# One 512-column product for the high part of U against both parts of x2, with the halves added afterwards, in a decoder layer's expert stage

## What is computed

```
q = (x @ w_pq)                      # 8 heads, two halves of 128
s1, s2 = q . sub_keys               # 128 scores each
idx, g = top 16 of the 256 sums of the two top-16 lists; g = softmax(top)
h = expert_u[idx] . x
a = g * gelu(h)
y = sum over the 8*16 picked of a * expert_v[idx]
```

## Time and profile before

| | before |
|---|---|
| median of 3 runs | 2499.41 us (2499.28 to 2500.96) |
| the profiled execution | 2502.8 us |
| its span | 2501.0 us |
| TensorE busy | 2409.1 us, 96% of the span |
| VectorE busy | 1548.8 us, 62% |
| ScalarE busy | 1019.1 us, 41% |
| GpSimd busy | 567.5 us, 23% |
| mean granted TensorE clock | 0.985 of full speed |

### The profile page before, as it was taken

One profiled execution on the slowest core, in us unless ns is written; L12 is line 12 of the kernel. 1 busy time (PEld: TensorE's weight loads), 2 busy tenths in 40 slices (PEclk: granted clock), 3 DMA queues, 4 the chain that ended last, 5 costly groups with the idle time before them and its releaser, 6 DMA issues.

```text
span 2501.0 us, 44448 instructions
## 1 busy us (share of the span) xinstructions
PE 2409.1 (96%) x14090; PEld 2158.2 (86%) x14090; DVE 1548.8 (62%) x2397; ACT 1019.1 (41%) x1586; POOL 567.5 (23%) x344
## 2 busy tenths in 40 slices
PE   7999999998999799999999999999799999999996
PEld 7988799877988699888889999999688888888885
DVE  4444566646434545777778888888355555555556
ACT  3444556533433342111134444444344444444442
POOL 0000000000110201777678788800000000000000
PEclk9999999999999899999999999999899999999998
DMA  8788554565444474777777777766766666666664
GB/s 308 251 277 272 165 152 135 165 239 168 158 145 161 144 180 104 154 151 153 151 155 182 184 182 183 182 183 182 205 214 218 217 218 213 219 216 219 213 220 139
DMA packets 342695, 473.74 MB, mean 189 GB/s; under 512 B 83153, under 2 KB 230865, under 8 KB 339313
## 3 DMA queue, kind: packets, MB, share of 16 engines
q1 hardware_dynamic: 301344, 446.81, 58.9%
q0 software_dynamic: 40592, 25.45, 6.4%
q10 hardware_dynamic: 704, 0.75, 0.1%
HBM read 451.77 MB, written 21.10 MB: 189 GB/s over the span
## 4 chain that ended last, share of the span: by engine, by line
PE 94%; DVE 2%; ACT 1%; issue 1%; SPq 1%; DMA 1%; POOL 0%; DVEq 0%; ACTq 0%; POOLq 0%
PE ps L660 28%; PE ps L638 18%; PE ps L427 18%; PE ps L433 15%; PE ps L627 13%; SPq L386 1%; PE ps L575 1%; PE ps L593 1%; DMA weight_ring<-in_w_in_dram 0%; DVE split_ring L1085 0%; PE ps L611 0%; DVE parts L1077 0%; ACT parts L719 0%; ACT split_ring L736 0%; PE ps L506 0%
## 5 line engine op out<-in xcount | busy, mean ns | idle before, releaser
L660 PE MATMUL ps<-parts,temp_parts 128*128 128x512 f32 x3072 | 701.0, 391 | 17.8 <-DVE parts L1407 17.8
L660 PEld LDWEIGHTS ps<-parts,temp_parts 128*128 128x128 f32 x3072 | 579.6, 189 | 139.0 <-issue 18.4
L1085 DVE TENSOR_TENSOR split_ring<-weight_ring,split_ring 128x1024 fp32r<-128x1024 f32 x288 | 353.0, 1233 | 389.0 <-ACT split_ring L736 381.1
L1054 POOL DMA_INDIRECT gates_scratch<-sbg x256 | 496.6, 1940 | 250.9 <-issue 132.6
L1407 DVE TENSOR_TENSOR parts<-region,parts 128x512 fp32r<-128x512 f32 x512 | 330.5, 687 | 288.0 <-ACT parts L944 287.9
L638 PE MATMUL ps<-parts,u_hi 128*128 128x256 f32 x2560 | 461.1, 283 | 0.3 <-DVE u_lo L1299 0.3
L736 ACT ACTIVATE split_ring<-weight_ring 128x1024 fp32r<-128x1024 f32 x288 | 303.2, 1059 | 370.0 <-PE ps L427 226.1
L427 PE MATMUL ps<-split_ring,parts 128*128 128x512 f32 x1920 | 439.9, 391 | 5.6 <-DVE parts L1201 3.9
L427 PEld LDWEIGHTS ps<-split_ring,parts 128*128 128x128 f32 x1920 | 360.8, 188 | 81.0 <-DVE split_ring L1085 4.1
L638 PEld LDWEIGHTS ps<-parts,u_hi 128*128 128x128 f32 x2560 | 399.4, 192 | 0.5 <-DVE u_lo L1299 0.5
L1293 DVE STREAM_TRANSPOSE u_turned<-u_raw 128x1024 f32<-128x1024 f32 x256 | 318.3, 1244 | 128.9 <-PE ps L627 43.1
(11 more groups left out here) (191 smaller groups left out, 956.9 us busy)
## 6 DMA issues: line engine op xcount, KB each, us to landing
u_raw<-in_peer_u_dram SPq DMA_DIRECT2D x1024, 128.0 KB
region<-in_peer_v_dram SPq DMA_DIRECT2D x256, 512.0 KB, 4.2
weight_ring<-in_w_in_dram SPq DMA_DIRECT2D x96, 512.0 KB, 5.1
weight_ring<-in_w_mkv_dram SPq DMA_DIRECT2D x64, 512.0 KB, 3.8
gates_scratch<-temps POOLq DMA_DIRECT2D x16, 1024.0 KB, 7.4
weight_ring<-in_w_o_dram SPq DMA_DIRECT2D x32, 512.0 KB, 3.9
weight_ring<-in_w_mq_dram SPq DMA_DIRECT2D x32, 512.0 KB, 3.6
weight_ring<-in_w_mo_dram SPq DMA_DIRECT2D x32, 512.0 KB, 3.6
```

The source lines that it names most:

```text
L660: m = nc.tensor.matmul(ps[:, 4 * t + q, :], e[:, c], v, start=first and n == 0, stop=False, skip_group_check=True)
L1054: pool.indirect_dma_start(gates_by_one, bass.IndirectOffsetOnAxis(ap=idx_all[:, j:j + 1], axis=0), gate_all[:, j:j + 1], None, compute_op= ...
L1085: nc.vector.tensor_tensor(w_lo[j % SPLIT], raw[j % RAW], w_hi[j % SPLIT].bitcast(F32), ALU.subtract).then_inc(lo_ready, 1)
```

## The change

`x_parts` is one tile over the two neighbouring regions that held the high part (`p1`) and the low part (`p3`) of x2, so that for each column group k an operand `x_both[:, k]` of 2 x 256 columns can be named: 256 of the high part, and 256 of the low part, which lie 4096 elements further on. In `split_unit`, `u_hi` multiplies both in one product of 512 columns: the high part's result goes to the bank's columns 0 to 255, the low part's to columns 256 to 511. `u_lo*x_hi` stays as it is and adds into columns 0 to 255. A unit is now 16 products, eight of 512 columns and eight of 256.

The two halves must be added. `take_hidden` is replaced, for the split blocks, by three steps: ACT copies columns 0 to 255 to `E` (`take_first`), DVE adds columns 256 to 511 (`add_halves`), ACT applies gelu in place (`take_summed`). The new semaphores `s_taken` and `s_summed` link them; `gelu_ready` is now given by the third step.

```diff
--- before.py
+++ after.py
@@ -101,7 +101,9 @@
                 5: RING + 6 * RC}
         TA = RING + 7 * RC
         r0, r1, r2, r3, r4, r5, r6 = [at(f"region{n}", HOME[n], RC) for n in range(7)]
-        p0, p1, p3, p4 = [at(f"parts{n}", HOME[n], RC, F32R) for n in (0, 1, 3, 4)]
+        p0, p4 = [at(f"parts{n}", HOME[n], RC, F32R) for n in (0, 4)]
+        x_parts = at("x_parts", HOME[1], 2 * RC, F32R)
+        p1, p3 = x_parts[:, 0:RC], x_parts[:, RC:2 * RC]
         ring = at("weight_ring", 0, RING)
         ta = at("temps", TA, TEMPS)
         ta_parts = at("temp_parts", TA, TEMPS, F32R)
@@ -150,6 +152,7 @@
         u_lo = [at(f"u_lo{s}", HOME[5] + (US + s) * UW, UW, F32R) for s in range(US)]
         u_hi = [at(f"u_hi{s}", HOME[5] + (2 * US + s) * UW, UW, F32R) for s in range(US)]
         xw = r0
+        x_both = x_parts[:, :].rearrange("p (n k t) -> p k n t", n=2, k=KB)
         E = at("experts", 0, NKEY * T)
         HALF, QTR = D // 2, D // 4
         v_raw = [r5[:, s * HALF:(s + 1) * HALF] for s in range(4)]
@@ -266,12 +269,12 @@
         top_ready, gexp_ready, gate_ready = sem("top_ready"), sem("gexp_ready"), sem("gate_ready")
         u_landed = [sem(f"u_landed{s}") for s in range(US)]
         u_turned, u_hi_ready, u_lo_ready, u_used = sem("u_turned"), sem("u_hi_ready"), sem("u_lo_ready"), sem("u_used")
-        gelu_ready = sem("gelu_ready")
+        gelu_ready, s_taken, s_summed = sem("gelu_ready"), sem("s_taken"), sem("s_summed")
         g_landed, e_scaled = [sem(f"g_landed{s}") for s in range(2)], sem("e_scaled")
         v_landed = [sem(f"v_landed{s}") for s in range(4)]
         e_hi_ready, e_lo_ready, v_hi_ready, v_lo_ready = sem("e_hi_ready"), sem("e_lo_ready"), sem("v_hi_ready"), sem("v_lo_ready")
         v_used = sem("v_used")
-        waited = sem("waited")
+        waited, waited_act = sem("waited"), sem("waited_act")
         y_ready, y_stored = sem("y_ready"), sem("y_stored")
 
 
@@ -634,9 +637,10 @@
                 for k in range(KB // 2):
                     kk = h * (KB // 2) + k
                     c = slice(k * P, (k + 1) * P)
-                    for n, (u, x) in enumerate(((u_hi[slot], x2T[0]), (u_hi[slot], x2T[1]), (u_lo[slot], x2T[0]))):
-                        m = nc.tensor.matmul(ps[:, b, 0:T], u[:, c], x[kk], start=kk == 0 and n == 0,
-                                             stop=kk == KB - 1 and n == 2)
+                    nc.tensor.matmul(ps[:, b, :].rearrange("p (n t) -> p n t", n=2), u_hi[slot][:, c], x_both[:, kk],
+                                     start=kk == 0, stop=False, skip_group_check=True)
+                    m = nc.tensor.matmul(ps[:, b, 0:T], u_lo[slot][:, c], x2T[0][kk], start=False, stop=kk == KB - 1,
+                                         skip_group_check=True)
                 m.then_inc(u_used, 1)
 
             def expert_block(unit_kind, i, b):
@@ -896,6 +900,18 @@
                 act.wait_ge(u_used, i * 2 + 2)
                 nc.scalar.activation(E[:, bass.ds(i * T, T)], ps[:, b, 0:T], ACT.Gelu).then_inc(gelu_ready, 1)
 
+            def take_first(i, b):
+
+                act.wait_ge(u_used, i * 2 + 2)
+                nc.scalar.activation(E[:, bass.ds(i * T, T)], ps[:, b, 0:T], ACT.Copy).then_inc(s_taken, 1)
+
+            def take_summed(i):
+
+                act.wait_ge(s_summed, i - (NATIVE // 2 - 1))
+                act.sem_inc(waited_act, 1)
+                now = E[:, bass.ds(i * T, T)]
+                nc.scalar.activation(now, now, ACT.Gelu).then_inc(gelu_ready, 1)
+
             def unit_hi(u, slot):
 
                 act.wait_ge(u_turned, u + 1)
@@ -918,12 +934,14 @@
             act.preload_act_table_set("gelu_and_others")
             with act.Fori(0, (UNITS - NATIVE) // 6) as n:
                 for b in range(3):
-                    for h in range(2):
-                        unit_hi(n * 6 + (NATIVE + 3 + 2 * b + h), (2 * b + h) % US)
-                    take_hidden(n * 3 + (NATIVE // 2 + b), b)
+                    unit_hi(n * 6 + (NATIVE + 3 + 2 * b), (2 * b) % US)
+                    take_first(n * 3 + (NATIVE // 2 + b), b)
+                    unit_hi(n * 6 + (NATIVE + 4 + 2 * b), (2 * b + 1) % US)
+                    take_summed(n * 3 + (NATIVE // 2 + b))
             unit_hi(UNITS - 1, (UNITS - 1) % US)
             for i in range(NKEY - NKEY % 3, NKEY):
-                take_hidden(i, i % 3)
+                take_first(i, i % 3)
+                take_summed(i)
 
             def expert_parts(i, b, first=False):
 
@@ -1298,6 +1316,12 @@
                 dve.wait_ge(u_hi_ready, u - (NATIVE - 1))
                 nc.vector.tensor_tensor(u_lo[slot][:, :], u_t[slot][:, :], u_hi[slot][:, :].bitcast(F32),
                                         ALU.subtract).then_inc(u_lo_ready, 1)
+
+            def add_halves(i, b):
+
+                dve.wait_ge(s_taken, i - (NATIVE // 2 - 1))
+                now = E[:, bass.ds(i * T, T)]
+                nc.vector.tensor_tensor(now, now, ps[:, b, T:2 * T], ALU.add).then_inc(s_summed, 1)
 
             def retrieve(n, turn):
 
@@ -1383,11 +1407,15 @@
                 for k in range(6):
                     u = NATIVE + US + k
                     turn_unit(n * 6 + u, u % US, n * 2 + (u // US + 1))
+                    if k % 2 == 1:
+                        add_halves(n * 3 + (NATIVE // 2 + k // 2), k // 2)
                     unit_lo(n * 6 + (u - 1), (u - 1) % US)
             u = UNITS - 1
             turn_unit(u, u % US, u // US + 1)
             unit_lo(u - 1, (u - 1) % US)
             unit_lo(u, u % US)
+            for i in range(NKEY - NKEY % 3, NKEY):
+                add_halves(i, i % 3)
 
             def scale(i, b):
 
```

## The result

The change makes the kernel slower: 2510.05 us, median of 7 executions (2506.95 to 2512.93), against 2500.79 for the kernel before in 7 (2499.28 to 2504.09); ratio 1.0037, 95% interval 1.0025 to 1.0048, so +9.3 us, 0.37%, with an interval of about 6 to 12. The profiled execution has a span of 2507.5 us (its time 2509.26), 6.5 more than that of before.

A forecast was written before the change was run, and what follows sets the result against it. TensorE was taken as the bound, with 0.33 us of slack per unit in VectorE's handover; 77 x 0.066 = 5.1, plus 0.06 at unit 99, less 0.3, gave +4.8 us: 2499.4 + 4.8 = 2504.2, range 2496 to 2513.

The forecast's parts named there:

- rival (b): TensorE's split products: a merged product costs as much as two, +13.1 us, 2512.5; chance 0.10.
- The chain of 3.17 us: From a unit's last product through turn, sum and lo to TensorE's effective start: 3.17 us instead of 2.90, once per block.
- The sign looked for: TensorE's record would show some 78 waits for `u_lo`, about 0.15 to 0.2 us, always at a block's second unit.
- the sum's place: On VectorE, 1.5 us after the unit's last product; ScalarE's copy would be done at 0.7, a margin of 0.8.
- rival (c): On VectorE, the sum doesn't slide between its neighbours or waits for the copy: 0.50 for 0.34, 2516.7; chance 0.05.
- Unit 99: Start of the counted periods in the split stretch: claimed to come only 0.06 us later than before.
- rival (a): At TensorE's wait, weights are fetched ahead, so it costs no weight load: 2496.4; chance 0.12.
- 0.347 for a pair: On TensorE, one 512-column and one 256-column product take 0.347 us for 0.360, so a unit takes 2.776 for 2.880.
- 5.826 for all: Each split block takes 5.826 us for 5.760, 0.066 longer, over 77 periods: 5.1 us.
- three units: After the last stall, three units end 0.104 us sooner each: -0.3 us.
- The end of the stretch: Copy, sum and gelu in a row delay the first V product about 1.0 us, hidden by a 14.76 us wait.

The follow-up runs named there:

- e3: The changed kernel with the sum on VectorE moved from in front of the low part (`lo`) to behind it: 2493.03 us, ratio 0.9960 to the kernel before.
- e8: The changed kernel with the merged product split into two of 256 columns and the sum behind the low part: 2501.30 us, ratio 0.9998 to the kernel before.
- e4: The changed kernel with a second, useless 256-column VectorE instruction beside the sum: 2537.57 us, ratio 1.0144 to the kernel before.
- e2: The changed kernel with the merged product split into two of 256 columns, sum still in front of the low part: 2512.09 us, ratio 1.0044.
- e5: The kernel of e3 with the 512-column operand read from one contiguous run (output not the layer's): 2487.51 us, ratio 0.9940 to the kernel before.
- e7: The changed kernel with products grouped by length and TensorE waiting for the low part only before the 256-column products: 2486.79 us, ratio 0.9943.
- e9: The kernel of e3, unchanged, traced three times more: 2484.38, 2491.91 and 2485.55 us.
- e6: The kernel of e3 with each unit's eight 512-column products first, then its eight of 256: 2490.53 us, ratio 0.9952 to the kernel before.

## Why the prediction came out as it did

The mechanism and its place were right, and the time lies inside the stated range of 2496 to 2513. It lies outside the narrower one of 2501.5 to 2507 that the prediction worked out for its own case, and closer to the 2512.5 of rival (b) than to the 2504.2 of the forecast: the trace gave +6.5 where the sum had +4.8, the medians +9.3.

- **VectorE's order, not its load, decides.** Shown: e3 exchanges two instructions of the changed kernel and turns its loss into a gain; e8 has the same work for nothing; VectorE is at 400.1 of 468.3 us in the stretch, 85%, and still the one who is late.
- **The chain of 3.17 us.** Measured 3.16. Its parts moved against each other: the sum takes 0.38, not 0.42, and `lo` starts 0.30 behind it, not 0.34, but `lo` behind a sum takes 1.21, not 1.18. The weight load that isn't ahead cost 0.11 (forecast 0.10). The sign looked for, 0.15 to 0.2 us of wait in the products' row, isn't there: the products' row lists next to nothing, and the loads' row 0.30.
- **Every instruction in front of `lo` costs its whole length.** e4: the late units start 0.34 later for one that stands 0.33.
- **The copy holds up the sum once.** In the steady state it is done 0.69 before the sum's place (forecast 0.8), and rival (c) is out for 77 of the 78. At the first split block ScalarE came late from two table loads of 1.28 us each, the copy ended at 1307.30, and the sum started at 1307.46 with `lo` 0.51 behind it, about rival (c)'s 0.50 for once:

```profile
1306.15 1.25 DVE L1311 STREAM_TRANSPOSE u_turned<-u_raw 128x1024 f32<-128x1024 f32 x1 [0.31 <-PE ps L642]
1306.94 0.36 ACT L906 ACTIVATE experts<-ps 128x256 f32 x1
1307.46 0.42 DVE L1324 TENSOR_TENSOR experts<-experts,ps 128x256 f32 x1
1307.97 1.23 DVE L1317 TENSOR_TENSOR u_lo<-u_turned,u_hi 128x1024 fp32r<-128x1024 f32 x1
```

  Unit 99 started 0.38 later than before and not 0.06: 0.3 of the missing 1.6 us.
- **The wait costs its weight load**: rival (a) is out, by the 0.34 between the first two products of every late unit.
- **The products: the term that was mis-sized.** The forecast took 0.347 for a pair, 0.227 + 0.120, from stretches in which all products have one length. In turns they fall into one of two rhythms, 0.347 or 0.353. In the profiled execution, worked out from all product starts, 39 of 77 blocks take 5.81 to 5.82 us and 38 take 5.85 to 5.87, the rhythm changing only where TensorE restarts behind a wait; forecast 5.826 for all. The mean of 5.841 is 0.015 x 77 = 1.2 of the missing 1.6 us; with unit 99's 0.3 and 0.1 at the end (three units, 0.2 sooner for 0.3) the sum closes. Rival (b), a pair at 0.360, had the right place and too large a size (its text has the loss over 8 us from 0.352; half the blocks at 0.353 brought 1.2): e2 shows that the merge does save time, and e5 that the two pieces don't matter.
- **The end of the stretch.** The first V product starts 1771.66 - 1767.35 = 4.31 behind the last split one, for 3.33 before, +0.98 (forecast 1.0), and the wait behind it takes it back:

```profile
1771.66 7.17 PE L664 MATMUL ps<-x_parts,temp_parts 128*128 128x512 f32 x24 [4.04 <-DVE x_parts L1435]
...
PE ps L664 <- DVE x_parts L1435: 17.9, 2, 13.8
```

  The wait is 13.8 for 14.8 us, as forecast; SP's 16 transfers (19.92 us after, from 1768.08) still set that date.
- **The size in medians.** Between the trace's +6.5 and the medians' +9.3 lie 2.8 us. A part is the granted clock, which differs between executions of one kernel in stages that the change doesn't touch: the kernel before took 2498.07 to 2500.43 us in the 12 executions recorded at 0.986 and 2500.68 to 2504.01 in the 13 at 0.984. At equal clock the changed kernel is 7 to 8 us slower: 2506.95 for a mean of 2498.9 at 0.986, 2508.8 for 2500.7 at 0.985, 2510.05 for 2502.9 at 0.984, 2512.5 for 2505.4 at 0.983 (the executions of before are those run beside the experiments, where the clock is on record; the chips may differ). Three of the seven fell to 0.983. The remaining 1 us or so is no more than what a clock given to 0.001 leaves open; more blocks in the slow rhythm would add up to 77 x 0.055 x one half = 2 us, which was not traced.

## What to carry to other kernels

Before an instruction is added to an engine that isn't the bound, look for the handover it stands in: count from the event that releases the engine to the date at which the bound engine wants the result. Here 0.33 us of slack per unit was the whole margin on an engine 81% busy, while behind the handover the same sum cost nothing (e3, e8). Where the bound engine has work that needs only a part of the operands, let it begin with that work and wait for the rest in the middle: that made the order on the other engine immaterial (e7). And a saving in products that is taken from stretches of equal products should be checked where the lengths alternate.

## What the runs showed of the hardware

- Products of 512 and of 256 columns in turns have two rhythms in one and the same program: 0.347 us a pair (0.230 + 0.117) or 0.353 (0.232 + 0.118, 0.240 + 0.120, 0.236 + 0.114 in turn). Each was kept for over 1200 pairs without a wait, and the stretches are 444.8 and 453.0 us (e9). The fast one gave way to the slow behind TensorE's loop without a wait, in both short traces. What decides between them was not found.
- Behind a change from 256 to 512 columns the next products stand up to 0.236 us apart and come to 0.227 only behind the fifth; behind a change from 512 to 256 the first two stand 0.113 apart instead of 0.120 (e6 and e7, worked out from the starts).
- A product that starts behind a wait is followed 0.10 to 0.11 us late by the next, with 512 columns (0.34 for 0.23, the changed kernel) as with 256 (0.22 for 0.12, e2); the row of the products hides this (0.6 us of waiting in the changed kernel's page), the row of the weight loads shows it (24.0 us).
